# A two-block transformer kernel: the first feed-forward with a second group of seven products

## The reference

```python
h = rmsnorm(x, norm_ffn[l])
x = x + (jax.nn.silu(h @ w_gate[l]) * (h @ w_up[l])) @ w_down[l]
```

## Time and profile before

| | us |
|---|---|
| median of 3 runs | 2477.63 |
| profiled execution, first to last instruction (span) | 2474.5 |
| PE busy | 2463.8 (100%) |
| DVE busy | 2105.3 (85%) |
| ACT busy | 1519.2 (61%) |
| POOL busy | 102.3 (4%) |
| chunk loop of the first feed-forward, one chunk | 62.2 |

### The profile page before, as it was taken

One profiled execution on the slowest core, in us unless ns is written; L12 is line 12 of the kernel. 1 busy time (PEld: TensorE's weight loads), 2 busy tenths in 40 slices (PEclk: granted clock), 3 DMA queues, 4 the chain that ended last, 5 costly groups with the idle time before them and its releaser, 6 DMA issues.

```text
span 2474.5 us, 28461 instructions
## 1 busy us (share of the span) xinstructions
PE 2463.8 (100%) x11266; PEld 2040.7 (82%) x11266; DVE 2105.3 (85%) x1724; ACT 1519.2 (61%) x1448; POOL 102.3 (4%) x96
## 2 busy tenths in 40 slices
PE   9999999999999999999999999999999999999998
PEld 7888888888888888888888888888888888888887
DVE  6977667988888888978788777777799999999997
ACT  7655556566666666665565565444566667766666
POOL 0000000000000000000000000000000000000000
PEclk9999999999999999999999999999999999999999
DMA  9536446677777777775455556557557777777775
GB/s 324 186 136 235 139 153 207 216 237 235 236 236 237 235 238 238 213 251 192 151 187 172 185 204 221 176 168 247 173 194 230 232 233 232 230 230 231 229 247 161
DMA packets 262756, 524.57 MB, mean 212 GB/s; under 512 B 9248, under 2 KB 9248, under 8 KB 262368
## 3 DMA queue, kind: packets, MB, share of 16 engines
q1 hardware_dynamic: 238976, 474.56, 55.8%
q0 software_dynamic: 22784, 46.62, 10.3%
q10 hardware_dynamic: 864, 1.57, 0.2%
HBM read 478.67 MB, written 2.10 MB: 194 GB/s over the span
## 4 chain that ended last, share of the span: by engine, by line
PE 99%; DVE 1%; DMA 0%; ACT 0%; issue 0%; SPq 0%; ACTq 0%; DVEq 0%
PE acc L862 23%; PE acc L866 23%; PE acc L864 23%; PE misc L862 6%; PE misc L866 6%; PE misc L864 6%; PE acc L879 1%; PE acc L875 1%; PE acc L877 1%; PE misc L907 1%; PE misc L915 1%; PE misc L875 1%; PE misc L879 1%; PE misc L877 1%; PE misc L998 0%; PE misc L978 0%
## 5 line engine op out<-in xcount | busy, mean ns | idle before, releaser
L1917 DVE TENSOR_TENSOR w_lo<-w_raw,w_hi 128x2048 fp32r<-128x2048 f32 (+1 forms) x473 | 1059.9, 2251 | 152.4 <-ACT w_hi L1384 151.0
L1384 ACT ACTIVATE w_hi<-w_raw 128x2048 fp32r<-128x2048 f32 (+1 forms) x473 | 892.0, 1890 | 345.5 <-PE acc L866 227.6
L862 PE MATMUL acc<-w_hi,xt_hi 128*128 128x512 f32 x1132 | 447.1, 395 | 0.2
L866 PE MATMUL acc<-w_hi,xt_lo 128*128 128x512 f32 x1132 | 441.3, 390 | 0.0
L864 PE MATMUL acc<-w_lo,xt_hi 128*128 128x512 f32 x1132 | 440.6, 389 | 0.0
L862 PEld LDWEIGHTS acc<-w_hi,xt_hi 128*128 128x128 f32 x1132 | 212.6, 188 | 44.7 <-issue 1.8
L866 PEld LDWEIGHTS acc<-w_hi,xt_lo 128*128 128x128 f32 x1132 | 212.4, 188 | 44.8
L864 PEld LDWEIGHTS acc<-w_lo,xt_hi 128*128 128x128 f32 x1132 | 212.7, 188 | 42.9
L1917 DVE TENSOR_TENSOR w_lo<-w_raw_more,w_hi 128x2048 fp32r<-128x2048 f32 (+1 forms) x99 | 221.8, 2240 | 30.1 <-ACT w_hi L1384 30.1
L1384 ACT ACTIVATE w_hi<-w_raw_more 128x2048 fp32r<-128x2048 f32 (+1 forms) x99 | 186.3, 1884 | 57.5 <-DVE w_raw_more L1887 15.8
L1891 DVE TENSOR_TENSOR w_raw<-w_raw 128x2048 f32<-128x2048 f32 x80 | 182.7, 2283 | 0.0
(11 more groups left out here) (388 smaller groups left out, 4189.8 us busy)
## 6 DMA issues: line engine op xcount, KB each, us to landing
w_raw<-in_w_in SPq DMA_DIRECT2D x132, 1024.0 KB, 5.1
w_raw<-in_w_ffn_up SPq DMA_DIRECT2D x61, 1024.0 KB, 6.6
w_raw<-in_w_ffn_down SPq DMA_DIRECT2D x42, 1024.0 KB, 5.7
x<-staged POOLq DMA_DIRECT2D x80, 512.0 KB, 6.2
w_raw<-in_w_out SPq DMA_DIRECT2D x32, 1024.0 KB, 5.1
w_raw<-in_w_gate SPq DMA_DIRECT2D x32, 1024.0 KB, 6.2
w_raw<-in_w_down SPq DMA_DIRECT2D x32, 1024.0 KB, 7.3
w_raw<-in_w_up SPq DMA_DIRECT2D x27, 1024.0 KB, 5.2
```

The lines of the kernel that those rows point to most:

```text
L862: nc.tensor.matmul(bank, hi[:, j, :], w_hi[:, t % RING, j, :], start=first and j == 0, stop=False, skip_group_check=shared)
L866: end = nc.tensor.matmul(bank, lo[:, j, :], w_hi[:, t % RING, j, :], start=False, stop=last and j == C - 1, skip_group_check=shared)
L1384: nc.scalar.activation(w_hi[:, t % RING, rows], raw_tile(steps[t].slot)[:, rows], ACT.Copy).then_inc(hi_ready, 1)
L1917: nc.vector.tensor_tensor(w_lo[:, t % RING, rows], raw_tile(steps[t].slot)[:, rows], w_hi[:, t % RING, rows].bitcast(F32), ALU.subtract).t ...
```

## The change

The chunk loop of the first feed-forward is written anew. The second feed-forward keeps its order.

- **Second group.** The third and fourth k-blocks of h (E steps, G3, U3) now go through a second group of seven half products, Q1 to Q7, of the same form as P. Both groups add into the same banks.
- **Seeded banks.** The seven products are arranged so that beta, gamma and zeta all start from alpha. ACT copies alpha into `misc` 0 after P1 and Q1, into `misc` 2 after P6 and Q6, into `misc` 1 after P7 and Q7 (`seeds`), and the later products add onto it. One ACT instruction per half then reads a bank and applies the silu. The up half needs two ACT copies and two DVE instructions (`second_up`, `first_up`).
- **Residual in PSUM.** ACT copies a quarter of `x` into the pair before a down step (`seed_x`), the down step adds onto it, and ACT copies the pair back into `x` (`x_back`). `staged` and the accumulating transfers are gone from this stage.
- **Fourth form of Q.** The weights of P4 and of Q5, Q6, Q7, P5, P6, P7 are summed by DVE. Those of Q4 are summed by one accumulating transfer per chunk from one raw slot to another, issued by POOL after the split of Q6 (`Added`).
- **Transposes.** The 8 transposes of a chunk stand together after the first step and go to `misc` 1 and 2.
- **Slots.** A seventh raw slot. The load of the final gain row is moved behind the chunk loop on POOL's queue.

```diff
-ORDER_WIDE = "P1 G3 P3 E1 D0 P5 E5 D1 E46 P6 U3 P7 P2 E73 D2 P4 D3".split()
-ORDER_WIDE_LAST = "P1 G3 E1 D0 P5 E5 U3 E46 P6 D1 E73 P2 P7 P4 P3 D2 D3".split()
+ORDER_TWO = "P1 Q1 P5 D0 Q5 D1 Q6 P6 P2 P7 Q7 Q3 P3 Q2 P4 D2 Q4 D3".split()
+ORDER_TWO_LAST = "P1 Q1 P5 D0 Q5 D1 Q6 P6 P2 P7 Q7 Q3 P3 Q2 P4 Q4 D2 D3".split()
...
+            release.update({g + "11": at[g + "4"], g + "12": at[g + "7"],
+                            g + "22": max(at[g + "3"], at[g + "6"] - 1, at[g + "7"] - 1),
+                            g + "21": max(at[g + "2"], at[g + "4"] - (g == "P"))})
...
+            if name == "Q4":
+                mine, other = (need(tile) for tile in forms[name])
+                added[at[name]] = Added(mine.slot, other.slot, other.count, at["Q6"], 1 + len(added))
+                steps.append(Step(mine.slot, None))
+            elif name in forms:
+                mine, other = (need(tile) for tile in forms[name])
+                sums[at[name]] = Sum(0, mine.slot, other.slot, other.count, at[name] - 1, "N" + name[1], None)
...
-        pool.wait_ge(tile_used, FFN1_T + 1)
+        for i in range(1, NF):
+            form = added[STEP[("ffn1", i), "Q4"]]
+            pool.wait_ge(lo_ready, form.after + 1)
+            pool.wait_ge(raw_ready[form.other], form.other_count)
+            pool.dma_start(raw_tile(form.slot), raw_tile(form.other), accum_op=ALU.add).then_inc(q4_added, 16)
+        pool.wait_ge(lo_ready, more_free[1] + 1)
         load(final_row[:], ins["norm_final"].partition_broadcast(P), row_loaded)
-        for i in range(1, NF):
-            for n in range(Q):
-                group_read(pool, ("ffn1_down", i - 1, n))
-                k = n % 2
-                pool.dma_start(x[:, :, n * N:(n + 1) * N], staged[k][:], accum_op=ALU.add).then_inc(staged_added[k], 16)
...
+        def set_bits():
+            bank_free(0, before["sums1", 1][0])
+            nc.tensor.matmul(misc[:, 0, :], xt_hi[:, 0, 0:P], xt_hi[:, 0:2, :], start=True, stop=True)
+        def seeded_iteration(i, after, within=None):
...
+                    pe.wait_ge(x_seeded, Q * (i - 1) + n + 1)
+                    products(t, both(pair_banks(pair_of(key)), ht_hi, ht_lo), first=False, shared=True,
+                             between=within and within.get(name))
...
+                if form in "62":
+                    pe.wait_ge(beta_seeded, i)
+                if form in "73":
+                    pe.wait_ge(zeta_seeded, i)
+                if form == "4":
+                    pe.wait_ge(gamma_seeded, i)
...
+        def seed_x(m):
...
+            pair, count = pairs["ffn1_down", i - 1, n]
+            act.wait_ge(pair_read[pair], count)
+            group_read(act, ("ffn1_down", i - 2, n) if i > 1 else ("down", 3, n))
+            copy(acc[:, pair], x[:, :, n * N:(n + 1) * N]).then_inc(x_seeded, 1)
+        def x_back(i, t, n):
+            pair = pair_of(("ffn1_down", i - 1, n))
+            act.wait_ge(tile_used, t + 1)
+            copy(x[:, :, n * N:(n + 1) * N], acc[:, pair]).then_inc(pair_read[pair], 1)
+            if i < NF - 1 or n == 0:
+                seed_x(Q * (i - 1) + n + 1)
+        def seeds(i, t, name):
...
+            if name == last_of(order, "P1", "Q1"):
+                act.wait_ge(drained[0], used[0])
+                act.wait_ge(tile_used, t + 1)
+                copy(misc[:, 0, :], alpha).then_inc(beta_seeded, 1)
...
+            if name == last_of(order, "P6", "Q6"):
+                act.wait_ge(drained[2], used[2])
+                act.wait_ge(tile_used, t + 1)
+                copy(misc[:, 2, :], alpha).then_inc(zeta_seeded, 1)
...
             if k == 2:
-                s_sums("ffn1", 1, a_sum, s_sum)
+                s_sums("ffn1", 1, a_sum, s_sum, 0, True)
             if k == 3:
-                wide_sums(1)
+                s_sums("ffn1q", 1, a_sum_q, s_sum_q, 2, True)
...
-                split(t + LEAD)
-                results_read(1, i, t, name, gate, hid)
-                if k in TURNS:
-                    hid_lo_half(i - 1, TURNS.index(k))
+                if k == 1:
+                    for half in range(2):
+                        hid_lo_half(i - 1, half)
+                split(t + LEAD, (lambda: gated_sums(i)) if i < NF - 1 and name == "D3" else None)
```

More of the change, by code:

```diff
@@ L227 @@
 Sum = namedtuple("Sum", "count slot other other_count made name after")
+Added = namedtuple("Added", "slot other other_count after count")
 def plan_weights():
-    loads, steps, sums, more_free = [], [], {}, {}
+    loads, steps, sums, more_free, added = [], [], {}, {}, {}
     free = [-1] * RAW_SLOTS
@@ L337, in plan_weights @@
         sums[t] = sums[t]._replace(count=count)
-    return loads, steps, sums, more_free
+    return loads, steps, sums, more_free, added
 def plan_pairs():
@@ L1143, in ffn_iteration @@
                         ready(i - 1)
-                    products(t, both(pair_banks(pair_of(key)), *((ht_hi, ht_lo) if ffn == 1 else (h2_hi, h2_lo))),
-                             between=within and within.get(name))
+                    products(t, both(pair_banks(pair_of(key)), h2_hi, h2_lo), between=within and within.get(name))
                 else:
@@ L1899, in split @@
                     weight_sum(later)
+            if between is not None:
+                between()
             if t >= STEPS:
                 return
-            if t not in sums and t >= FIRST:
+            if t not in sums and t not in added and t >= FIRST:
                 dve.wait_ge(raw_ready[steps[t].slot], steps[t].count)
```

235 lines of the change are left out of this document (173 added, 62 removed).

## The result

The changed kernel takes 2487.94 us (median of 4 runs, 2486.64 to 2488.82), the kernel before on the same chip 2477.64 (4 runs): a ratio of 1.0041, with a 95% interval of 1.0028 to 1.0054. The forecast was 2464.4, faster. The profiled execution's span is 2485.8 us in place of 2474.5.

The account below looks back on a forecast made before the run. PE was taken as the bound, the time being a count of matmuls. A gain of 14.0 us on PE less 0.8 in the first chunk made 13.2, so 2477.6 became 2464.4 us, range 2462.0 to 2474.5.

Parts of the forecast that it names:

- PE, the term that pays: First feed-forward's chunks: 264 matmuls instead of 270 and cheaper transposes, 14.0 us less on PE, a chunk of 60.75 us.
- DVE's work: Chunk of the first feed-forward: DVE has 58.7 us of work in 60.75, 97%, and it fits.
- ACT's seeds: ACT's copies into PSUM banks: 1.03 us each, between 0.67 and 1.91, with 0.26 us left at D1 and D3.
- rival 2: No gain: waits of 0.8 to 1.9 us a chunk, for which a 1.91 us seed is enough; 2472.7 to 2482.6, chance 0.09.
- rival 1: Short places at D1, D3, Q2 and P7 wait a little, 0.1 to 0.8 us a chunk: 2465.5 to 2472.5, chance 0.32.
- Transfers: Loads and Q4's addition in a chunk: addition hidden, 10 to 21 us within 23; P2's and Q2's tiles land within 6.9.
- The loads of P2's and Q2's tiles: Two late loads in a chunk, each issued 6.9 us before ACT wants it, taken to land in 5.1.
- Rival 3: Slower: P2's and Q2's tiles land in 10.6 us instead of 5.1, 15 us slower, 2493; it and its like 0.09.
- C: Follow-up theory, not in the forecast: traffic of the 1 MB addition in the first feed-forward slows the weight loads.
- The first chunk: Loads issued some 4 us later after Q1's split: up to 1.5 us of wait, once, 0.8 taken.

Follow-up runs that it names:

- e1: The changed kernel without the transfer that adds Q4's raw tiles and without ACT's wait for it, Q4 left unsummed: 2466.49 us.
- e2: The changed kernel with the addition reading the constant activation `xt_hi`, so without its wait for Q2's tile; same size and place, another number: 2464.99 us.
- e3: The changed kernel with half the addition (512 KB), same place and waits, the other half of Q4's weights unsummed; a single run: 2468.22 us.
- e9: As e4, but in the nine chunks before the last DVE sums Q4's form one split earlier, ahead of P4's split: 2468.24 us.
- e10: e9 together with e7's edit (low part of Q's activation sums one split later ahead of the first chunk), nothing left out: 2465.65 us.
- e4: The changed kernel with the two fourth forms exchanged: P4's weights summed by the transfer, Q4's by DVE, complete computation: 2471.04 us.
- e6: As e4, but in the nine chunks before the last DVE sums Q4's form behind D2's split, Q2's tile released one step later: 2480.8 us.
- e7: As e6, but the low part of Q's activation sums on DVE stands one split later ahead of the first chunk: 2479.39 us.

## Why the prediction was wrong

**Step by step.**
- *PE, the term that pays: right.* A chunk of 264 matmuls and eight transposes took the 60.75 us of the forecast in e1, e2 and e3, and 60.72 to 60.77 in all middle chunks of e9 and e10 but the fourth. Ten chunks of it are there to be had.
- *DVE's work: right in size.* 58.7 us a chunk forecast; 411.99 us in seven chunks of the changed kernel are 58.9 each:

```profile
573.01:1010.51 437.50, 431.89 (x1906) 349.96 (x1905) 411.99 (x212) 324.84 (x245) 5.95 (x7) 1.00 0.65 218
```

- *ACT's seeds: right.* `acc<-x` of 1024 took 1.03 us; rival 2, which needed 1.91, fell. The nine waits of PE for a seed come from ACT being late since Q4's high part: they are absent in e1, e2, e4 and e10, with the same seeds. They stand at D3, one of the two short places that the forecast named (0.26 us left), so rival 1's "a late DVE makes ACT late, which makes the seed late" had the right path to PE and the wrong start of it.
- *Transfers: this step failed.* It said: "The addition starts after Q6's split (18.6 + 1.2 of POOL), and ACT needs its result at 42: 23 us for something whose half lands in 5.0 to 10.6". The addition has two waits in the diff, and I worked out one. The other, `raw_ready[form.other]`, is Q2's tile, and two sentences later I placed the release of that very tile after P7's split (29.8) with a landing of 5.1. Put together, the two give 34.9 at the earliest. Measured: 36.6. With my own bound of 10 to 21 us for the landing that is 44.9 to 55.9 against a need at 42, readable from what stood in the text. The need at 42 was too strict: e3 started that high part at 45.2 and its chunk lost nothing. So at the lower bound the lateness would have been free; the landing of 11.9 after 36.6 was not (48.5).
- *The loads of P2's and Q2's tiles: Q2's right in size.* In the chunk shown it landed within 5.7 us (issue 791.88, addition released at 797.54), though not alone: SP issued others at 794.08 and 796.34. Rival 3, the slower one, named this tile and the right direction, but had it land late for its own split; its price (15 us slower at a landing of 10.6, no loss below 9.1) belongs to another mechanism than the one that acted. Its sign, waits of ACT `w_hi` for DMA, came, but from the addition. Its 0.09 was too low a chance for all that hung on these transfers.
- *The landing of the addition.* Issued in a quiet stretch it takes 7.0 us in the median (e2, e4), issued between SP's loads 11.9. The changed kernel's windows (DMA share is the number before the last):

```profile
782.00:790.00 8.00, 8.00 (x37) 6.63 (x36) 8.00 (x5) 5.53 (x5) 0.00 (x0) 1.00 0.01 2
790.00:798.00 8.00, 7.97 (x36) 6.28 (x35) 8.00 (x4) 6.71 (x5) 0.46 (x1) 1.00 0.64 215
798.00:810.00 12.00, 12.00 (x55) 9.86 (x54) 9.99 (x6) 6.36 (x6) 0.38 (x1) 1.00 1.01 277
```

The DMA engines had almost nothing to do for 8 us (a share of 0.01), and the addition was issued as they became full. ACT waited 4.92 us in this chunk, and 11.9 less 7.0 is 4.9: at this late moment a landing of 7.0 would have been just in time for ACT. Lateness and contention act in series, and the first brings the second. The Trainium skill (DMA: Bandwidth & Descriptors, Issuing engines are not separate DMA queues) says that transfers started by different engines run on the same 16 DMA engines and interleave; the 7.0 and 11.9 agree with it, and so do the loads, whose median landing went to 11.0. C saw one half of this, the loads slowed by the addition; the half that cost time is the addition slowed by the loads.
- *The first chunk: right in kind.* 0.8 us were taken; PE waited 1.0 + 0.3 there, in e2 too, and moving one DVE instruction of 2.2 us took out the wait for `ht_lo` and 1.4 us of time (e6 to e7).

**Where the 23.5 us between forecast and result are.** Up to the transposes of `x` after the loop the changed kernel (1090.42) is 21.7 us later than e2 (1068.73), the kernel that the prediction described: 2.1 up to the end of the first chunk (510.28 against 508.17), 14.3 in the eight middle ones (500.23 against 485.96), 5.3 in the last. The first of these holds a scatter from ahead of the loop, where the programs are the same: e1, which has no addition, is at 510.24 as well, since its loop began 2.0 us later than e2's. Counted from the loop's start the first chunk costs the changed kernel 2.75 us against e2. The remaining 1.8 us: the spans differ by 21.5, and the medians by more (2487.9 and 2465.0, not run side by side).

**What of the sum itself stays open.** e2's median of 2464.99 lies 12.0 us under the runs of before beside it (2477.01), where 13.2 were expected. The forecast took 3.1 us between span and median; in every run on record since, time and span of the same execution lie 1.7 to 2.0 us apart, so the rest of the 3.1 should be the difference between one execution and the median. That cancels in the forecast of the median, but the span of 2461.3 was too low by it: e2's spans are 2463.1 to 2464.3. The eight middle chunks gave their 11.4 us; what stands ahead of them and behind them up to the transposes of `x`, which should have given some 2, lost 0.8 against before. The waits in the first chunk are 1.3 us of that. The range had a slip too: it goes to 2474.5, "where rival 2 begins to hold", while rival 2 begins at 2472.7. The last chunk's order is another one in each kernel, and I didn't follow up the rest.

## What to carry to other kernels

When a transfer or an instruction has several waits, write the earliest time of each from the plan, take the latest, and only then ask whether the rest of the path hides it. On an engine that works in order the due time of an input is not when its own result is needed but when everything queued behind it must start: check what a late input holds up (5 us of waiting at one high part cost 1.5 to 1.8 us a chunk, by a seed that stands behind it and two more high parts). Give the transfer those operands that are there early and leave the late pair to the engine that stands next to its use; here that exchange and the place of one sum turned 2488 us into 2466.
